# Sharing PSUM banks among the seven products of an FFN pair, with partial sums read between products

## The reference

```python
h = rmsnorm(x, g_ffn_pre)
f = (jax.nn.silu(h @ w_ffn_gate) * (h @ w_ffn_up)) @ w_ffn_down
x = x + rmsnorm(f, g_ffn_post)
x = x + (p @ w_ple_proj) * jax.nn.sigmoid(x @ w_ple_gate)
```

## Time and profile before

| | us |
|---|---|
| median of 3 runs (981.18 to 981.36) | 981.26 |
| span of the profiled execution, first to last instruction | 980.1 |
| TensorE busy (matmuls, modelled ends) | 973.4 |
| VectorE busy | 631.8 |
| ScalarE busy | 397.5 |
| GpSimd busy | 85.7 |

### The profile page before, as it was taken

How to read it: one execution, slowest core, us unless ns; L and a number is a source line. 1 busy time by engine, 2 the same in 40 slices (tenths; PEclk the granted TensorE clock), 3 DMA queues, 4 the chain that set the end, 5 groups by cost and what they waited for, 6 DMA issues and landing times.

```text
span 980.1 us, 18694 instructions
## 1 busy us (share of the span) xinstructions
PE 973.4 (99%) x7286; PEld 954.4 (97%) x7286; DVE 631.8 (64%) x1248; ACT 397.5 (41%) x699; POOL 85.7 (9%) x140
## 2 busy tenths in 40 slices
PE   9999999999999999999999999999999999999998
PEld 7999999999999999999999999999999999999997
DVE  5554676757665633435458899625997469975772
ACT  5334533434343522223455555424453234544352
POOL 2123212112100000010003000000000000030000
PEclk9999999999999999999999999999999999999999
DMA  8434221222222232246603533521334213366221
GB/s 215 136 111 133 82 67 55 66 76 67 60 69 66 76 90 83 76 127 183 185 2 116 208 85 88 150 66 45 108 102 124 77 45 108 101 196 198 87 55 45
DMA packets 166245, 98.68 MB, mean 101 GB/s; under 512 B 14688, under 2 KB 162560, under 8 KB 165904
## 3 DMA queue, kind: packets, MB, share of 16 engines
q1 hardware_dynamic: 159936, 79.19, 28.6%
q0 software_dynamic: 4336, 16.67, 4.9%
q10 hardware_dynamic: 1888, 1.64, 0.6%
HBM read 86.79 MB, written 10.75 MB: 100 GB/s over the span
## 4 chain that ended last, share of the span: by engine, by line
PE 98%; DMA 0%; DVE 0%; ACT 0%; issue 0%; SPq 0%; DVEq 0%; ACTq 0%
PE acc L697 37%; PE acc L977 11%; PE acc L978 11%; PE acc L979 11%; PE small L977 6%; PE small L978 6%; PE small L979 6%; PE small L846 1%; PE small L892 1%; PE small L863 1%; PE small L896 1%; PE small L855 1%; PE small L894 1%; PE acc L808 1%; PE small L781 1%; PE small L877 1%
## 5 line engine op out<-in xcount | busy, mean ns | idle before, releaser
L697 PE MATMUL acc<-xh,whi 128*128 128x288 f32 x720 | 158.7, 301 | 0.2
L697 PE MATMUL acc<-xl,whi 128*128 128x288 f32 x720 | 153.4, 294 | 0.0
L697 PE MATMUL acc<-xh,wlo 128*128 128x288 f32 x720 | 153.4, 294 | 0.0
L1166 ACT ACTIVATE whi<-raw 128x1024 fp32r<-128x1024 f32 (+1 forms) x60 | 60.0, 1001 | 197.3 <-PE acc L697 196.1
L697 PEld LDWEIGHTS acc<-xh,whi 128*128 128x128 f32 x720 | 114.0, 188 | 5.7 <-issue 4.7
L697 PEld LDWEIGHTS acc<-xh,wlo 128*128 128x128 f32 x720 | 115.0, 188 | 0.0
L697 PEld LDWEIGHTS acc<-xl,whi 128*128 128x128 f32 x720 | 114.9, 188 | 0.0
L2008 DVE TENSOR_TENSOR wlo<-raw,whi 128x512 fp32r<-128x512 f32 (+2 forms) x93 | 80.9, 871 | 49.9 <-ACT whi L1387 34.1
L977 PE MATMUL acc<-yh,whi 128*128 128x288 f32 x360 | 107.0, 297 | 0.0
L979 PE MATMUL acc<-yh,wlo 128*128 128x288 f32 x360 | 106.1, 295 | 0.0
L1675 DVE TENSOR_TENSOR wlo<-raw,whi 128x1024 fp32r<-128x1024 f32 (+1 forms) x62 | 71.8, 1157 | 44.3 <-ACT whi L1166 43.4
(11 more groups left out here) (337 smaller groups left out, 2399.0 us busy)
## 6 DMA issues: line engine op xcount, KB each, us to landing
raw<-in_w_in SPq DMA_DIRECT2D x91, 256.0 KB, 3.2
raw<-in_w_ffn_gate SPq DMA_DIRECT2D x44, 256.0 KB, 3.4
raw<-in_w_ffn_up SPq DMA_DIRECT2D x44, 256.0 KB, 4.1
raw<-in_w_ffn_down SPq DMA_DIRECT2D x32, 256.0 KB, 3.6
res<-x_scratch POOLq DMA_DIRECT2D x16, 288.0 KB, 4.2
raw<-in_w_branch_ret SPq DMA_DIRECT2D x16, 256.0 KB, 3.0
raw<-in_w_out SPq DMA_DIRECT2D x16, 256.0 KB, 4.6
raw<-in_w_ffn_down SPq DMA_DIRECT2D x16, 192.0 KB, 3.8
```

What stands on the lines that cost most here:

```text
L697: ins = nc.tensor.matmul(acc[:, a, hf, 0:HALF], w[:, s, at:at + P], x(k)[:, hf * HALF:(hf + 1) * HALF], start=first and n == 0 and m == 0, ...
L1166: nc.scalar.activation(whi[:, s, 0:n], raw[:, s, 0:n], ACT.Copy).then_inc(hi_ready, 1)
```

## The change

Each pair uses three banks instead of seven, and even and odd pairs take turns between banks 0 to 2 and 3 to 5 (`PAIR_BANK`, to which 3 is added for odd i). PA0, PS2, PS3 and PB1 share one bank; PS2, PS3 and PB1 add to what stands there (`ADDED`, start=False), so the bank holds PA0, then PA0 + PS2, then that + PS3, then up r0. PS1 and PS4 share another bank, PA1 has the third. PS3 now comes before PS4. ScalarE copies PA0, PS1 and PA0 + PS2 out to `kept`, each before the next product on that bank may open it. VectorE adds three times per pair (`add_kept`: after PS3 into `up`, PA1 and PS4 into `zt`), and `f_out` multiplies in two halves of 288 columns, the second straight out of PSUM. ScalarE's `f_high` also waits for that second half. Nothing else of the program is altered; DMAs and matmuls are as many as before.

```diff
-PA0, PS1, PS2, PA1, PS4, PS3, PB1 = range(PRODUCTS)
+PA0, PS1, PS2, PA1, PS3, PS4, PB1 = range(PRODUCTS)
+PAIR_BANK = {PA0: 0, PS2: 0, PS3: 0, PB1: 0, PA1: 1, PS1: 2, PS4: 2}
+ADDED = (PS2, PS3, PB1, PS4)
...
         if e[0] == "prod":
-            b = e[2]
+            b = PAIR_BANK[e[2]] + 3 * (e[1] % 2)
...
-S_STEP = {PS1: 0, PS2: 1, PS4: 2, PS3: 3}
+S_STEP = {PS1: 0, PS2: 1, PS3: 2, PS4: 3}
...
-                    ins = triple(e, weight(e, k), x_h[:, k, :], x_l[:, k, :], k == 0, k == KD // 2 - 1)
+                    ins = triple(e, weight(e, k), x_h[:, k, :], x_l[:, k, :], k == 0 and t not in ADDED,
+                                 k == KD // 2 - 1, t in ADDED)
...
                 act.wait_ge(f_ready, i - PLAIN + 1)
+                p4 = ("prod", i, PB1)
+                act.wait_ge(bank_read[BANK[p4]], TURN[p4] + 1)
...
-                if t == PA0:
-                    copy_out(e, kept[:, 0, :])
+                if t in (PA0, PS1, PS2):
+                    copy_out(e, kept[:, (PA0, PS1, PS2).index(t), :])
...
-            def u_sums(i):
...
-            def gate_sum(i):
...
-            def up_late(i):
...
+            def add_kept(i, t, dst, n):
+
+                e, copied = ("prod", i, t), ("prod", i, (PA0, PS1, PS2)[n])
+                dve.wait_ge(bank_read[BANK[copied]], TURN[copied] + 1)
+                dve.wait_ge(pe_done, EVENT[e])
+                nc.vector.tensor_tensor(dst, bank_of(e), kept[:, n, :], ALU.add).then_inc(bank_read[BANK[e]], 1)
 
             def f_out(i):
 
-                n = i - PLAIN
                 p4, p7 = ("prod", i, PB1), ("prod", i, PS3)
+                dve.wait_ge(gate_ready, i - PLAIN + 1)
+                dve.wait_ge(f_lo, PLAIN + i)
+                dve.wait_ge(bank_read[BANK[p7]], TURN[p7] + 1)
+                nc.vector.scalar_tensor_tensor(ta[:, cols(1)], up[:, cols(1)], -1.0, tb[:, cols(1)], ALU.mult,
+                                               ALU.mult).then_inc(f_ready, 1)
                 dve.wait_ge(pe_done, EVENT[p4])
...
+                nc.vector.scalar_tensor_tensor(ta[:, cols(0)], bank_of(p4), -1.0, tb[:, cols(0)], ALU.mult,
+                                               ALU.mult).then_inc(bank_read[BANK[p4]], 1)
...
-                if t == PS2:
-                    u_sums(i)
+                if t == PS3:
+                    add_kept(i, PS3, up[:, cols(1)], 1)
                 elif t == PS4:
-                    gate_sum(i)
-                elif t == PS3:
-                    up_late(i)
+                    add_kept(i, PS4, zt[:, 1, cols(1)], 2)
...
+                if t == PS3:
+                    add_kept(i, PA1, zt[:, 1, cols(0)], 0)
```

More of the change, by code:

```diff
@@ L262, in bank_turns @@
     bank, turn = {}, {}
-    used = [0] * PRODUCTS
+    used = [0] * 6
     n = 0
@@ L467, in encoder_layer @@
         pe_done = sem("pe_done")
-        bank_read = [sem(f"bank_read{b}") for b in range(PRODUCTS)]
+        bank_read = [sem(f"bank_read{b}") for b in range(6)]
         init_done = sem("init_done")
@@ L525, in acc_of @@
             return acc[:, a, :, 0:HALF]
-        banks = [acc[:, b // 2, b % 2, 0:HALF] for b in range(4)] + [small[:, 512 * b:512 * b + HALF] for b in range(3)]
+        banks = [acc[:, b // 2, b % 2, 0:HALF] for b in range(4)] + [small[:, 512 * b:512 * b + HALF] for b in range(2)]
         side = [small[:, 1024 + 512 * h:1536 + 512 * h] for h in range(2)]
@@ L972, in weight, with triple @@
                 return hi[:, s % 2, at:at + P], lo[:, s % 2, at:at + P]
-            def triple(e, weights, x_h, x_l, first, last):
+            def triple(e, weights, x_h, x_l, first, last, added=False):
                 (w_h, w_l), bank = weights, bank_of(e)
-                nc.tensor.matmul(bank, w_h, x_h, start=first, stop=False)
-                nc.tensor.matmul(bank, w_h, x_l, start=False, stop=False)
-                return nc.tensor.matmul(bank, w_l, x_h, start=False, stop=last)
+                nc.tensor.matmul(bank, w_h, x_h, start=first, stop=False, skip_group_check=added)
+                nc.tensor.matmul(bank, w_h, x_l, start=False, stop=False, skip_group_check=added)
+                return nc.tensor.matmul(bank, w_l, x_h, start=False, stop=last, skip_group_check=added)
             def open_bank(e):
@@ L984, in open_bank @@
                     pe.wait_ge(bank_read[b], TURN[e])
-                elif b == PB1:
-                    pe.wait_ge(yn_ready, 2 * KD)
                 elif b < 4:
@@ L1516, in first_products @@
             def first_products(i, n):
-                for t in ((PA0, PS1), (PS2, PA1), (PS4, PS3), (PB1,))[n]:
+                for t in ((PA0, PS1), (PS2, PA1), (PS3, PS4), (PB1,))[n]:
                     hi(("prod", i, t))
@@ L1551, in product_out @@
                     hi(("down", KD * group_of(i) + (1, 3, 5, 6).index(t)))
-                if t == PS3:
+                if t == PS4:
                     for p in (PA1, PS4):
@@ L2197, in product_operand @@
                 elif t == PS2:
+                    sum_of(i, PS3)
+                elif t == PA1:
                     sum_of(i, PS4)
-                elif t == PA1:
-                    sum_of(i, PS3)
                 lo(("prod", i, t))
             def first_products(i, n):
-                for t in ((PA0, PS1), (PS2, PA1), (PS4, PS3), (PB1,))[n]:
+                for t in ((PA0, PS1), (PS2, PA1), (PS3, PS4), (PB1,))[n]:
                     product_operand(i, t)
@@ L2223, in f_low @@
                 nc.vector.tensor_tensor(fl[:, n, :], ta[:, :], fh[:, n, :].bitcast(F32), ALU.subtract).then_inc(f_lo, 1)
-            def u_sums(i):
-                p1, p5, p6 = (("prod", i, t) for t in (PA0, PS1, PS2))
-                n = i - PLAIN
[L2230 to L2234, removed]
@@ L2251, in f_out @@
             def f_out(i):
-                n = i - PLAIN
                 p4, p7 = ("prod", i, PB1), ("prod", i, PS3)
-                dve.wait_ge(pe_done, EVENT[p4])
[L2256 to L2261, removed]
+                dve.wait_ge(gate_ready, i - PLAIN + 1)
```

## The result

The kernel after takes 988.13 us (median of five runs, 987.82 to 988.59) against 981.36 us of the kernel before on the same chip (981.18 to 981.45): ratio 1.0068, interval 1.0058 to 1.0079. It is slower by 6.8 us; the forecast was 987.3, range 984.3 to 990.8.

The account below looks back on a forecast made before the run. TensorE was taken as the bound, VectorE right behind. Waits of 3.51, 1.68 and 0.79 us sum to 5.98 on the 980.1 us span; with 1.2 us around it that gives 987.3 us, range 984.3 to 990.8.

Parts of the forecast that it names:

- TensorE bounds, a lighter VectorE gives nothing: Steady pairs: TensorE never waits at 11.13 us a pair, so taking about 1.3 us off VectorE gains nothing.
- Rival (c): All pairs: less VectorE and ScalarE traffic speeds the matmuls, so not slower, 980.9 us at a 0.1285 us pitch; chance 0.02.
- The openings that add onto a bank just read: Four per pair, 19 pairs: first matmuls take the usual 0.1325 us; bounds -0.8 to +0.8 us in all.
- Steady pairs: New bank waits in steady pairs are met without cost, with margins of 0.85 and 0.76 us.
- Rival (a): Steady pairs wait too, from 0.8 us of lateness on; 0.3 us beyond it in 19 pairs gives 993.0; chance 0.10.
- First pair: Pair i = 3: three waits of 2.25, 0.90 and 0.36 us, together 3.51; the last alone sets it.
- End of pair 14: First down projection product reopens bank 0 and waits for f_out's half products: 1.68 us, bounds 1.4 to 2.1.
- Start of pair 15: PA0 reopens bank 3, just filled by the last down product, and waits for VectorE's addition: 0.79 us.
- The sum: Whole run: 5.98 us of waits on the 980.1 us span, plus 1.2 us around it, gives 987.3 us.
- Rival (b): After the five waits TensorE's clock falls, one product at 1.2 GHz each: 8 us more, 995.2; chance 0.03.
- Rival (d): Queues of ScalarE or VectorE run earlier, part of the waits is absent, only the first pair costs: 984.8 or less; chance 0.05.

Follow-up runs that it names:

- the bank experiment: Kernel after with the last silu's plain half product (4,1) before pair 3 in bank 0 instead of bank 3: 987.99 us, ratio 1.0067.

## Why the prediction was right

**TensorE bounds, a lighter VectorE gives nothing: right.** The pair stays at 11.13 us with VectorE 1.35 us lighter; predicted were about 9.5 and 6.5 us for the two engines, measured 9.43 and 6.45. Rival (c), not slower because of less traffic, falls with it.

**The openings that add onto a bank just read: right, at nothing.** 11.13 us holds four of them. The 0.8 us kept on either side for them were not needed.

**Steady pairs: right.** Margins predicted 0.85 and 0.76, read 0.84 and 0.71; in them 0.60 us of lateness stayed hidden and 1.0 us came through with 0.32. Rival (a) needed only 0.8 us more lateness than there was: the kernel with the addition 1.0 us later is that rival, and took 993.17 us where (a) said 993.0, though in 14 pairs and not in 19.

**First pair: mechanism and size right.** 2.25, 0.90, 0.36 became 2.27, 0.83, 0.31. The sentence that the last wait alone sets the delay is shown by the bank experiment, where two of the three waits changed and the sum did not. What the prediction did not see is that behind the last wait stands another: with all three removed, pair 4 waits for what VectorE could not finish in the time TensorE no longer gave it. Of the 3.6 us that they cost with their restarts, 1.9 were won and 1.7 came back there. VectorE is without idle time there (4.00 of the 4.00 us from 574 to 578 us) in the kernel after and in the one without the three waits alike, so it gets through its weight operations no sooner when TensorE stops waiting; the first waits had given it time to catch up.

**End of pair 14: right, 0.10 us high.** Predicted 1.68, measured 1.58. The half product takes 0.45 us and lets the next start after 0.37, where the prediction took 0.51 from a gain multiplication and 0.42 from the overlap of additions.

**Start of pair 15: right,** 0.79 against 0.80.

**The sum: two small terms missing.** 5.98 was predicted and 5.79 measured for the delays; the restart of 0.07 us after each wait, 0.35 in all, was not in the sum. 6.14 us stand against a difference of median spans of 986.0 - 979.7 = 6.3. The other term is what lies around the span, carried over as 1.2 us: the profiled execution of before had a span 0.4 us above the median one, and executions of the kernel before stand some 1.8 us above their own span, those with shared banks 2.1 to 2.3. These 0.3 us remain with all edge waits gone and in no order-only kernel (1.83), so they go with the shared banks, but what they are stays open: no view covers time outside the span. That the range holds 988.13 is in part luck: without the room kept for the openings and for the start of rival (a), neither of which cost anything, it would have ended at 987.7.

**Rival (b), the clock: wrong as a forecast, but not empty.** In the profile after, the granted clock is 1.00 throughout 560 to 580 us. Of the other kernels' profiles, two show it at half once around pair 3, after a wait of 2.1 to 2.4 us; the price was about 1 us once where (b) had 8. That bears out the Trainium skill's page "TensorE: Matmul & The Clock Gate", section "A second HAM failure mode: psum-queue depth-cycling", so far as idle time at banks can cost clock; the repeated swinging between half and full that it tells of is in no run here.

The evidence that the prediction held against (b) was weaker than it looked. Timeline of TensorE in the kernel before:

```profile
1.11 4.63 PE L764 MATMUL acc<-ones 128*128 128x128 f32 x20 [1.11 <-DVE rowsum L1686]
...
8.30 1.38 PE L764 MATMUL acc<-ones 128*128 128x128 f32 x10
```

The same matmul took 0.23 us early on and 0.14 us later (0.21 and 0.11 us from start to start), though the clock reads 1.00 all the while. The early pace held until 6.9 us, so the 1.00 of the earlier trace rows cannot be relied on for the first 1.9 us of its window. From 7 to 10 us TensorE kept the faster pace, with idle times of up to 0.64 us.

**Rival (d), part of the waits absent:** all five were there.

## What to carry to other kernels

When banks are shared, ask at every reopening who reads the bank last and what stands ahead of that reader in its queue; the steady loop may have 0.7 us to spare while the first pass and the edges between phases, where the banks come in another order, have none. Waits that follow each other on one engine can be one delay, set by the last of them, as in pair 3 here: count that one, and before removing it look for the one behind. Work taken off an engine that is not the bound bought nothing here, 1.35 us in each of 19 pairs.

## What was not expected of the hardware

TensorE's granted clock fell, in some executions, after a wait of over 2 us in the middle of otherwise full work. Windows of the kernel with the exchanged banks, after its 2.36 us wait for `kept` that ended at 573.83 (columns as the earlier trace rows):

```profile
575.00:576.00 1.00, 1.00 (x7) 1.00 (x7) 1.00 (x3) 0.75 (x2) 0.00 (x0) 0.65 0.98 269
576.00:577.00 1.00, 1.00 (x6) 1.00 (x5) 1.00 (x3) 0.63 (x1) 0.00 (x0) 0.50 0.46 132
577.00:578.00 1.00, 1.00 (x6) 1.00 (x5) 1.00 (x3) 0.00 (x1) 0.00 (x0) 0.50 0.01 2
578.00:579.00 1.00, 1.00 (x6) 1.00 (x6) 0.39 (x2) 0.00 (x0) 0.00 (x0) 0.64 0.00 0
579.00:580.00 1.00, 1.00 (x10) 1.00 (x9) 0.88 (x2) 0.62 (x2) 0.00 (x0) 1.00 0.00 0
```

The granted clock is 0.50, that is 1.2 GHz, for some 3 us, and the busy share reads full all the while; the granted clock and the count of matmuls (six or seven in a microsecond instead of nine or ten) tell. The kernel with the addition 0.6 us later shows the same after its 2.1 us wait for silu:

```profile
568.00:569.00 1.00, 1.00 (x7) 1.00 (x6) 1.00 (x3) 0.17 (x1) 0.00 (x0) 0.59 0.00 0
569.00:570.00 1.00, 1.00 (x6) 1.00 (x5) 1.00 (x3) 0.76 (x2) 0.00 (x0) 0.50 0.00 0
570.00:571.00 1.00, 1.00 (x6) 1.00 (x6) 1.00 (x2) 0.00 (x0) 0.00 (x0) 0.50 0.00 0
571.00:572.00 1.00, 1.00 (x7) 1.00 (x7) 1.00 (x3) 0.29 (x1) 0.00 (x0) 0.70 0.00 0
```

There it cost nothing: PB1 waits for VectorE's addition on PS3 anyway, and starts 0.15 us after its end. The profile after, with a wait of the same 2.1 us, kept 1.00.

The mean granted clock of each run says how often. Five kernels have a wait of over 2 us in pair 3 (the kernel after, the one with the down projection on other banks, the one with exchanged banks, and the two with the later addition): 12 of the 24 runs counted here have a mean of 0.997 or 0.998, 12 have 0.999 or 1.000. No run of any other kernel here is below 0.999. With the exchanged banks the three runs near 990.7 us have 0.998 and the two faster ones 0.999; with the down projection on other banks four of five runs have 0.997 or 0.998, and take 985.5 to 986.1 us against 985.43 of the fifth. What decides between one run and the next is open.
